# Three transformer blocks in one program: a joined change to the opening, the end, the norms, the linear attention's order, and the convolution's taps on quarters of TensorE

## The chip, the cores and the metric

The program runs on one NeuronCore of one Trainium2 chip. The metric is the device time in microseconds of one execution. The core's engines are TensorE (PE; its weight loads are listed apart as PEld), VectorE (DVE), ScalarE (ACT), GpSimd (POOL) and SyncE (SP), which issues nearly all DMAs. Each engine runs its own stream of instructions in order, and they meet through semaphores.

## What is computed

The input x is 256 tokens by 1024 features, float32. Two layers of a first model and one of a second follow, 8 stages in the kernel's count:

```python
# stages 0, 2, 3, 5: feed-forward;  1: even_mixer;  4: odd_mixer
for l in range(2):
    f = swiglu(rms_norm(h, g[0]), ffn1_w_in[l], ffn1_w_out[l])
    h = h + 0.5 * rms_norm(f, g[1])
    m = even_mixer(rms_norm(h, g[2]), ...) if l == 0 else odd_mixer(rms_norm(h, g[2]), ...)
    h = h + rms_norm(m, g[3])
    f = swiglu(rms_norm(h, g[4]), ffn2_w_in[l], ffn2_w_out[l])
    h = h + 0.5 * rms_norm(f, g[5])
# even_mixer: 8 heads of stick-breaking attention beside
c = u * sigmoid(gate)                      # 512 channels
c = causal_depthwise_conv(c, dw_w, dw_b)   # 31 taps for each channel
c = silu(layer_norm(c, ln_g, ln_b))
m = concat([attention, c]) @ hyb_w_out
# odd_mixer: gated linear attention, 4 heads
o = rms_norm(gla(q, k, v, g), norm_g);  m = (o * silu(r)) @ gla_w_out
# stages 6, 7: a second block (sparse attention, retention, gated feed-forward),
# its norms modulated by a scale and a shift, and at the end
out = rms_norm(x + gate2 * ffn, final_norm_w)
```

## The kernel before, in words

**Matrix products.** Every float32 weight matrix is streamed from HBM in units of 1 MB (`load_unit`, L429), three buffers `raw` deep. A unit holds two sub-blocks of 2 x 128 rows by 512 columns. For each, ACT rounds it to fp32r (`whi`, L460) and DVE makes the rest (`wlo`, L469). The activations are split alike into `xh` (ACT, L775) and `xl` (DVE, L770). PE then makes three products of 512 columns for each 128 rows: xh·whi (L571), xh·wlo (L572), xl·whi (L574). One sub-block for one half of the tokens (`tok` 0 or 1, 128 tokens) is a part (`pe_part`, L576): six matmuls. `act_begin` and `dve_begin` run the splits a few sub-blocks ahead.

**Order of work.** The order on every engine is written out by hand. At the entry of a stage (`pe_first`, L601) the parts of tok 0 come first while tok 1 is still being normed: PE transposes h (L743), DVE multiplies by the gain (L764), ACT and DVE split. The factor 1/rms (`rstd`) is applied later, when PSUM is read. It is made by ACT (sum of squares, L683) and by three POOL instructions: add the two halves (L697), scale and add epsilon (L690), power -0.5 (L692). In stages 6 and 7 (`pe_ada_x`, `act_ada_x`, `dve_ada_x`) it is applied before the transposes (L1681), then scale and shift (L1694, L1707).

**Opening (stage 0).** PE waits for the constants, transposes the norm gains (L555) and x (L743). DVE and ACT make all of tok 0's `xh` and `xl`, then split four sub-blocks; PE does parts 0 to 3 of tok 0, and tok 1's transposes before part 3.

**Stage 1 (`pe_hyb`, L1112).** The convolution has 4 blocks of 128 channels by 31 taps. A tap is either one DVE instruction (L1241, `Y += w_k * shifted x`) or one PE matmul with a diagonal 128x128 weight matrix that POOL made (L1108, L1311). PE has 38 taps (block 3, and 7 of block 2, `NT = 24`), DVE 86. All are float32, and a float32 matmul leaves two records in the trace. PE's taps stand in six groups between the attention's steps: weights (L1059, L1060), values (L1077, L1078, two heads on the two halves of PE's columns), scores (L1021, L1029, L1033, two heads on the two halves of PE's rows). Then come the mean (L1096), the variance (L1096 again), rsqrt and silu on ACT (L1223 to L1232), and the product with `hyb_w_out` (`pe_down`), whose part 4 is the first to need the silu's result.

**Stage 4 (`pe_gla`, L1473).** The scores of the chunked linear attention are made in 9 levels. `GLA` (L1342) is the hand-written order of their steps in 12 slots, one before each part pair of projections 3 to 6: "a" (POOL, differences), "e" (ACT, exp), "m" (DVE or POOL, times q and k), 0 and 1 (PE's two dots, L1391, and DVE's masked copies, L1435). After projection 6, eight heads' outputs (L1505, L1508) are made one to a PSUM bank, squared, normed (L1641), gated (L1644), transposed (L743) and split.

**End.** For each tok: DVE multiplies by the gate row (L1770), adds h (L1773), ACT squares, POOL makes rstd, DVE scales two halves (L2439), SP stores each (L2500).

## Time and profile before

| | |
|---|---|
| device time, median of 3 runs | 1450.81 us (1449.68 to 1451.09) |
| the profiled execution's own time | 1449.5 us |
| its span, first to last instruction | 1447.7 us |
| PE busy | 1418.4 us, 98% |
| DVE, ACT, POOL busy | 945.8, 720.4, 165.5 us |
| mean DMA rate | 198 GB/s |

In the rows below a time is in us from the span's start. A timeline row has start, length, engine, line, operation, out<-in, shapes, count, and in brackets the idle time before it and what ended it. Consecutive instructions of one form are merged (x8). Matmuls are pipelined, so the length of one (0.39) is longer than the step to the next (0.23). What a matmul costs in a stream is that step, or the whole of a merged row by its count.

### The profile page before, as it was taken

What the parts mean: (1) busy time and instruction counts of PE and PEld (TensorE: products, weight loads), DVE (VectorE), ACT (ScalarE), POOL (GpSimd) and SP (SyncE); (2) the same over time, 40 slices, a digit from 0 to 9 for tenths busy, and PEclk for the clock granted to TensorE, in tenths of its full rate; (3) what the DMA queues carried; (4) which work ended last, traced back from release to release, by engine and by line L of the source; (5) the groups of instructions that cost most, each with busy time, mean ns of one, the idle gap of its engine ahead of it and who ended that gap; (6) DMA issues with size and microseconds to landing.
All of it is one profiled execution on the core that took longest, in us unless ns stands there. A gap on an engine that the chain in (4) does not pass through costs nothing.

```text
span 1447.7 us, 17857 instructions
## 1 busy us (share of the span) xinstructions
PE 1418.4 (98%) x6695; PEld 1170.0 (81%) x6695; DVE 945.8 (65%) x1321; ACT 720.4 (50%) x1054; POOL 165.5 (11%) x262
## 2 busy tenths in 40 slices
PE   7999999999999999999999999999999999999997
PEld 5888888778888888888888888887877788788886
DVE  5666667777665677665786776665468566655543
ACT  5454455565444455543754544445555634544442
POOL 1900010010000010000162100001542110100000
PEclk9999999999999999999999999999999999999999
DMA  8685755246876778768533588674845355465551
GB/s 282 201 256 202 261 198 202 66 145 191 247 231 214 251 233 260 244 216 263 204 121 124 169 222 264 229 238 144 216 161 204 118 175 174 160 204 175 182 207 62
DMA packets 236341, 286.50 MB, mean 198 GB/s; under 512 B 37028, under 2 KB 160464, under 8 KB 236256
## 3 DMA queue, kind: packets, MB, share of 16 engines
q1 hardware_dynamic: 236000, 285.25, 61.1%
q8 instruction: 53, 0.87, 0.2%
q14 instruction: 32, 0.26, 0.1%
q10 hardware_dynamic: 256, 0.11, 0.0%
HBM read 281.13 MB, written 4.20 MB: 197 GB/s over the span
## 4 chain that ended last, share of the span: by engine, by line
PE 91%; ACT 3%; DVE 3%; DMA 2%; issue 2%; POOL 0%; ACTq 0%; DVEq 0%; POOLq 0%
PE ps L571 28%; PE ps L574 27%; PE ps L572 27%; PE ps L857 2%; DMA raw<-in_w_in_dram 1%; PE ps L1108 1%; PE ps L743 1%; ACT whi L460 1%; DVE wlo L469 1%; PE ps L1391 1%; PE ps L1059 0%; ACT junk L683 0%; PE ps L996 0%; ACT xh L775 0%; DMA fold<-in_norm_g_dram 0%
## 5 line engine op out<-in xcount | busy, mean ns | idle before, releaser
L469 DVE TENSOR_TENSOR wlo<-raw,whi 128x1024 fp32r<-128x1024 f32 (+2 forms) x474 | 563.1, 1222 | 243.9 <-ACT whi L460 243.5
L460 ACT ACTIVATE whi<-raw 128x1024 fp32r<-128x1024 f32 (+2 forms) x474 | 471.9, 1042 | 235.7 <-PE ps L574 95.3
L571 PE MATMUL ps<-whi,xh 128*128 128x512 f32 (+2 forms) x1440 | 567.9, 394 | 9.2 <-DVE wlo L469 6.7
L572 PE MATMUL ps<-wlo,xh 128*128 128x512 f32 (+2 forms) x1440 | 555.4, 386 | 0.0
L574 PE MATMUL ps<-whi,xl 128*128 128x512 f32 (+2 forms) x1440 | 548.3, 386 | 0.0
L571 PEld LDWEIGHTS ps<-whi,xh 128*128 128x128 f32 x1440 | 271.0, 188 | 67.8 <-DVE wlo L469 9.3
L574 PEld LDWEIGHTS ps<-whi,xl 128*128 128x128 f32 x1440 | 270.7, 188 | 55.6
L572 PEld LDWEIGHTS ps<-wlo,xh 128*128 128x128 f32 x1440 | 271.2, 188 | 50.7
L571 PE MATMUL ps<-whi,gh 128*128 128x512 f32 x440 | 172.6, 392 | 0.0
L572 PE MATMUL ps<-wlo,gh 128*128 128x512 f32 x440 | 171.3, 389 | 0.0
L574 PE MATMUL ps<-whi,gl 128*128 128x512 f32 x440 | 153.5, 389 | 0.0
L697 POOL TENSOR_TENSOR st<-st 128x1 f32<-128x1 f32 x30 | 8.2, 272 | 1094.9 <-ACT junk L683 1094.3
L838 ACT ACTIVATE hid<-ps,st 128x256 f32<-128x256 f32 x88 | 41.4, 471 | 126.2 <-PE ps L574 124.9
L574 PEld LDWEIGHTS ps<-whi,gl 128*128 128x128 f32 x440 | 82.6, 188 | 17.4
L572 PEld LDWEIGHTS ps<-wlo,gh 128*128 128x128 f32 x440 | 82.7, 188 | 16.7
L571 PEld LDWEIGHTS ps<-whi,gh 128*128 128x128 f32 x440 | 82.6, 188 | 16.7
L844 DVE SCALAR_TENSOR_TENSOR hid<-ps,st,hid 128x256 f32<-128x256 f32 x88 | 42.2, 479 | 62.2 <-ACT hid L838 62.2
L868 DVE TENSOR_TENSOR gl<-ps,gh 128x512 fp32r<-128x512 f32 x55 | 38.0, 691 | 67.1 <-ACT gh L863 67.1
L863 ACT ACTIVATE gh<-ps 128x512 fp32r<-128x512 f32 x55 | 32.9, 598 | 74.7 <-PE ps L857 74.7
L489 DVE SCALAR_TENSOR_TENSOR adaacc<-adat,scol,adaacc 128x512 f32<-128x512 f32 x84 | 62.9, 748 | 0.0
L775 ACT ACTIVATE xh<-xtmp 128x512 fp32r<-128x512 f32 x32 | 19.4, 634 | 32.9 <-DVE xtmp L764 32.7
L1311 POOL TENSOR_SCALAR diag<-cst,vcol 128x128 f32<-128x128 f32 x38 | 34.1, 916 | 7.9 <-DVE vcol L562 7.9
(239 smaller groups left out, 915.7 us busy)
## 6 DMA issues: line engine op xcount, KB each, us to landing
raw<-in_ffn_w_in_dram SPq DMA_DIRECT2D x174, 512.0 KB, 5.4
raw<-in_ffn_w_out_dram SPq DMA_DIRECT2D x40, 1024.0 KB, 5.7
raw<-in_w_in_dram SPq DMA_DIRECT2D x26, 1024.0 KB, 4.9
adat<-in_w_ada_dram SPq DMA_DIRECT2D x96, 256.0 KB, 2.9
raw<-in_w_ffn_gate_dram SPq DMA_DIRECT2D x22, 512.0 KB, 3.9
raw<-in_w_ffn_up_dram SPq DMA_DIRECT2D x22, 512.0 KB, 4.9
raw<-in_hyb_w_in_dram SPq DMA_DIRECT2D x10, 1024.0 KB, 5.5
raw<-in_gla_w_in_dram SPq DMA_DIRECT2D x10, 1024.0 KB, 5.1
```

The source lines that it names most:

```text
L460: e.activation(split_of(whi, j), raw_of(j), ACT.Copy).then_inc(*whi_made.up(j))
L469: e.tensor_tensor(split_of(wlo, j), raw_of(j), split_of(whi, j).bitcast(F32), ALU.subtract).then_inc(*wlo_made.up(j))
L489: e.scalar_tensor_tensor(adaacc[:, :], adat[n % 2][:, :], sc, adaacc[:, :], ALU.mult, ALU.add).then_inc(*ada_added.up(c, k))
L571: e.matmul(ps[:, 0:n], a, whi_of(j, k), start=first and k == 0, stop=False)
L572: last = e.matmul(ps[:, 0:n], a, wlo_of(j, k), start=False, stop=False)
L574: last = e.matmul(ps[:, 0:n], b, whi_of(j, k), start=False, stop=final and k == subs[j][2] - 1)
L838: e.activation(hb[:, tok * 512 + 256:tok * 512 + 512], acc.of(st, J0[st] + 4 * c, tok)[:, 0:256], ACT.Silu, scale=rstd(("h", st, tok)) if ...
L844: e.scalar_tensor_tensor(hb[:, tok * 512:tok * 512 + 256], acc.of(st, J0[st] + 4 * c, tok)[:, 256:512], rstd(("h", st, tok)) if st < 7 els ...
L857: last = e.transpose(ps[:, j * 256 + tok * P:j * 256 + (tok + 1) * P], hb[:, tok * 512 + j * P:tok * 512 + (j + 1) * P], ident)
L863: e.activation(gh[:, c * 512:(c + 1) * 512], tb.of("hid", st, c)[:, :], ACT.Copy).then_inc(*ghi_made.up(st, c))
L868: e.tensor_tensor(gl[:, c * 512:(c + 1) * 512], tb.of("hid", st, c)[:, :], gh[:, c * 512:(c + 1) * 512].bitcast(F32), ALU.subtract).then_i ...
L1311: e.tensor_scalar(diag[:, i * P:(i + 1) * P], ident, conv_w(b, k), None, ALU.mult).then_inc(*diag_made.up(i))
```

## The change

- **Opening.** PE runs 10 float32 matmuls on a tile of ones before the gains' transposes and 4 after the first x transposes (`pe_warm`). ACT's table set is loaded at once. Sub-blocks 0 and 1 are split before the second half of tok 0's `xh` and `xl`; tok 1 is turned before part 1, and the parts alternate between tok 0 and tok 1. The first part starts with the products that need only `whi` and `xh` (`pe_opening`).
- **Norms.** POOL's three instructions become two; the scale is put into ACT's squares.
- **Convolution.** PE takes 42 taps (`NT = 20`), DVE 82. A tap is two matmuls of 64 rows by 64 columns. Taps of even number use the quarters (rows 0-63, columns 0-63) and (64-127, 64-127) and sum in one PSUM bank, the odd ones the two other quarters and a second bank with its halves swapped. ACT copies the second bank, and two more matmuls with the identity swap it back into the first (`pe_taps_join`). The variance is asked for one pair of parts earlier (`i == 2`).
- **Linear attention.** Step (1, "m") moves from slot 4 to slot 3. ACT makes all Abs before Exp and Ln. The outputs go two heads to a bank, are made before parts 2 and 3 of projection 6, and half of tok 0's operand is transposed there; DVE gates two heads at once.
- **Stages 6 and 7.** `xh` and `xl` are made and waited for in four pairs of blocks, not two halves.
- **End.** The last tok's first half is multiplied by the gain ahead and scaled by ACT, which stores it through its own queue, beside DVE and SP with the other half.

The core of the diff:

```diff
+        def pe_warm(e, n):
+            e.wait_ge(*ones_set.at())
+            for _ in range(n):
+                e.matmul(acc.tiles[5][:, 0:P], ones[:, :], ones[:, :], start=True, stop=True)
...
-            lead = {0: 4, 6: 7, 7: 7}.get(st, 6)
+            lead = {6: 7, 7: 7}.get(st, 6)
...
-                return order + [(i, tok) for i in range(4, 8) for tok in range(2)]
+                return [(0, 0), (1, 0), (0, 1), (1, 1)] + [(i, tok) for i in range(2, 8) for tok in range(2)]
...
         def pool_rstd(e, key, factor=1.0):
-            e.tensor_tensor(v, ss[:, 0:1], ss[:, 1:2], ALU.add).then_inc(*rstd_step.up(key, 0))
-            e.wait_ge(*rstd_step.at(key, 0))
-            pool_power(e, v, 1, 1.0 / D, key, factor)
+            e.tensor_scalar(wk, ss[:, 0:1], ss[:, 1:2], EPS * factor ** -2, ALU.add, ALU.add
+                            ).then_inc(*rstd_step.up(key, 1))
+            e.wait_ge(*rstd_step.at(key, 1))
+            e.tensor_tensor(rk, wk, mhalf[:, 0:1], ALU.pow).then_inc(*rstd_made.up(key))
...
-        NT = 24
+        NT = 20
...
-                t = e.matmul(tb.of("conv")[:, (b - 2) * 256:(b - 1) * 256], diag[:, i * P:(i + 1) * P], cx_of(b, k),
-                             start=i == 0, stop=k == 30, skip_group_check=True)
+                ps = tb.of("convx" if i % 2 else "conv")
+                for p in (slice(0, 64), slice(64, P)):
+                    q = slice(64 - p.start, P - p.start) if i % 2 else p
+                    t = e.matmul(ps[q, (b - 2) * 256:(b - 1) * 256], diag[p, i * 64:(i + 1) * 64], cx_of(b, k)[p, :],
+                                 start=i < 2, stop=i % 2 == 1 and k >= 29, skip_group_check=True)
...
+        def pe_taps_join(e):
+            e.wait_ge(*convx_made.at())
+            for p in (slice(0, 64), slice(64, P)):
+                q = slice(64 - p.start, P - p.start)
+                t = e.matmul(tb.of("conv")[q, :], ident[p, p], hid[1][p, 0:512], start=False, stop=True,
+                             skip_group_check=True)
+            t.then_inc(*conv_sum.up())
...
+            pe_taps(e, PE_TAPS[36:42])
             pair(pe_values, 2)
-            pe_taps(e, PE_TAPS[32:38])
             pair(pe_values, 3)
+            pe_taps_join(e)
...
+            e.wait_ge(*conv_dot.at())
+            e.activation(hid[1][:, 0:512], tb.of("convx")[:, :], ACT.Copy).then_inc(*convx_made.up())
             act_values(e, 2)
-            e.wait_ge(*conv_dot.at())
+            e.wait_ge(*conv_sum.at())
...
-        GLA = [(1, "m"), (4, "a"), (3, "e"), (2, "m")]
+        GLA = [(4, "a"), (3, "e"), (2, "m"), "-"]
...
+                    if c == 6 and i >= 2:
+                        for hp in range(2):
+                            pe_gla_out(e, i - 2, hp)
+                    if c == 6 and i == 3:
+                        operand(0, 0)
...
+            e.activation(h[:, D:D + 512], xtmp[:, 0:512], ACT.Copy, scale=rstd(("h", 8, 1))).then_inc(*out_scaled.up())
+            e.wait_ge(*out_scaled.at())
+            e.dma_start(out[0, P:2 * P, 0:512], h[:, D:D + 512]).then_inc(*s_out_act.up())
```

## Rows read from the trace of the kernel before

**Rows 1.** The page: busy time by engine, and the granted clock in 40 slices.

```profile
PE 1418.4 (98%) x6695; PEld 1170.0 (81%) x6695; DVE 945.8 (65%) x1321; ACT 720.4 (50%) x1054; POOL 165.5 (11%) x262
...
PEclk9999999999999999999999999999999999999999
```

**Rows 2.** Waits of PE: engine, line, releaser: us in total, times, longest.

```profile
PE ps L571 <- DVE wlo L469: 6.7, 5, 3.7
PE ps L555 <- DMA fold<-in_norm_g_dram: 4.9, 1, 4.9
PE ps L743 <- ACT hid L1681: 2.5, 3, 1.1
PE ps L571 <- ACT xh L1232: 2.0, 2, 1.7
PE ps L1391 <- DVE gX L1420: 1.7, 1, 1.7
...
PE ps L743 <- DVE gr L1644: 1.1, 1, 1.1
```

**Rows 3.** Timeline of the opening, all engines.

```profile
5.09 1.91 PE L743 MATMUL ps<-cst,h 128*128 128x128 f32 x8
...
6.99 0.63 ACT L775 ACTIVATE xh<-xtmp 128x512 fp32r<-128x512 f32 x1 [4.06 <-DVE xtmp L764]
...
8.30 1.99 ACT L460 ACTIVATE whi<-raw 128x1024 fp32r<-128x1024 f32 x2
9.37 2.36 DVE L469 TENSOR_TENSOR wlo<-raw,whi 128x1024 fp32r<-128x1024 f32 x2 [0.26 <-ACT whi L460]
...
10.65 0.80 PE L571 MATMUL ps<-whi,xh 128*128 128x512 f32 x1 [3.65 <-DVE wlo L469]
...
13.38 0.63 PE L571 MATMUL ps<-whi,xh 128*128 128x512 f32 x1
...
13.81 0.63 PE L572 MATMUL ps<-wlo,xh 128*128 128x512 f32 x1
```

**Rows 4.** Timeline of PE around 26 us.

```profile
25.83 0.50 PE L571 MATMUL ps<-whi,xh 128*128 128x512 f32 x1 [1.30 <-DVE wlo L469]
```

**Rows 5.** Timeline of PE in stage 1: scores, taps, weights, values.

```profile
254.00 0.70 PE L1029 MATMUL ps<-qT,kT 64*128 64x256 f32 x4
...
261.79 3.62 PE L1108 MATMUL ps<-cx,diag 128*128 128x256 f32 x16
265.24 0.81 PE L1059 MATMUL ps<-mb,cst 128*128 128x384 f32 x2
...
271.40 0.66 PE L1077 MATMUL ps<-eb,vt 128*64 128x256 f32 x4
```

**Rows 6.** Chain that ended last, transposes of stage 1's entry (start, us, what).

```profile
198.97 0.87 PE ps L743 x8
```

**Rows 7.** Timeline of DVE in stage 1.

```profile
265.21 10.37 DVE L1241 SCALAR_TENSOR_TENSOR Y<-cx,vcol,Y 128x256 f32<-128x256 f32 x26
...
293.29 0.42 DVE L1287 TENSOR_TENSOR Y<-ps,Y 128x256 f32<-128x256 f32 x1
```

**Rows 8.** Timeline of PE at the end of stage 1: the mean, part 4.

```profile
294.48 1.89 PE L1096 MATMUL ps<-Y,ones 128*128 128x256 f32 x8
...
307.95 0.47 PE L571 MATMUL ps<-whi,xh 128*128 128x512 f32 x1 [1.68 <-ACT xh L1232]
```

**Rows 9.** Timeline of PE in stage 4: the outputs.

```profile
785.21 2.32 PE L1505 MATMUL ps<-gv,gS 128*128 128x256 f32 x10
```

**Rows 10.** Timeline of POOL at stage 7's entry: one rstd.

```profile
1246.14 0.19 POOL L697 TENSOR_TENSOR st<-st 128x1 f32<-128x1 f32 x1 [63.65 <-ACT junk L683]
1246.41 0.19 POOL L690 TENSOR_SCALAR st<-st 128x1 f32<-128x1 f32 x1
```

**Rows 11.** Timeline of the end.

```profile
1443.82 1.41 DVE L2439 SCALAR_TENSOR_TENSOR h<-h,st,row 128x512 f32<-128x512 f32 x2 [1.97 <-POOL st L692]
1444.60 0.99 SPq L2500 DMA_DIRECT2D out_dram<-h  x2
```

More of the change, by code:

```diff
@@ L616, in pe_first, with pe_opening @@
                         e.wait_ge(*done)
-                new = (xhi_made.at(st, tok, k // 2), xlo_made.at(st, tok, k // 2)) if c == 0 and k % 2 == 0 else ()
-                pe_part(e, bank[c, tok], j0 + i, xh, xl, 2 * k, 8, tok, *new)
+                new = ()
+                if c == 0 and (st >= 6 or k % 2 == 0):
+                    x = (st, tok, k if st >= 6 else k // 2)
+                    new = xhi_made.at(*x), xlo_made.at(*x)
+                if (st, i, tok) == (0, 0, 0):
+                    pe_opening(e, bank[c, tok], *new)
+                else:
+                    pe_part(e, bank[c, tok], j0 + i, xh, xl, 2 * k, 8, tok, *new)
+        def pe_opening(e, ps, hi, lo):
+            n = subs[0][3]
+            e.wait_ge(*whi_made.at(0))
+            e.wait_ge(*hi)
+            for k in range(2):
+                e.matmul(ps[:, 0:n], x_block(xh, k, 0), whi_of(0, k), start=k == 0, stop=False)
+            e.wait_ge(*lo)
+            for k in range(2):
+                e.matmul(ps[:, 0:n], x_block(xl, k, 0), whi_of(0, k), start=False, stop=False)
+            e.wait_ge(*wlo_made.at(0))
+            for k in range(2):
+                last = e.matmul(ps[:, 0:n], x_block(xh, k, 0), wlo_of(0, k), start=False, stop=False)
+            last.then_inc(*mm[0].up(0))
         def pe_chunk(e, st, j0, readers, at=None):
@@ L1275, in dve_hyb @@
             logs(1)
-            some(26)
+            some(20)
+            logs(2)
             dve_values(e, 0)
-            logs(2)
             some(6)
@@ L1281, in dve_hyb @@
             dve_values(e, 1)
-            some(8)
+            some(11)
             dve_values(e, 2)
@@ L1515, in pe_gla, with pe_gla_out @@
                     if q % 4 == 0 else (),
-                    lambda tok, n: [(squares, ("f", 4, tok), n), (f_scaled, 4, tok, n)], late=lambda: operand(1),
+                    lambda tok, n: [(squares, ("f", 4, tok), n), (f_scaled, 4, tok, n)], second, late,
                     lag=LAG[4], then=entry(e, 5))
+        def pe_gla_out(e, tok, hp):
+            ps = acc.next(("out", tok, hp), (gla_gated, tok, hp))
+            for done in acc.freed:
+                e.wait_ge(*done)
+            if (tok, hp) == (0, 0):
+                e.wait_ge(*lv_put.at(7, 1))
+                e.wait_ge(*lv_put.at(8, 0))
+                e.wait_ge(*gla_in.at(4, 1))
+            for hd in (2 * hp, 2 * hp + 1):
+                z = ps[:, hd % 2 * 256:hd % 2 * 256 + 256]
+                t = e.matmul(z, gS[:, hd * 256 + tok * P:hd * 256 + (tok + 1) * P],
+                             gv[:, tok * D + hd * 256:tok * D + (hd + 1) * 256], start=hd % 2 == 0, stop=tok == 0,
+                             skip_group_check=True)
+                if tok:
+                    t = e.matmul(z, gOFF[:, hd * P:(hd + 1) * P], gv[:, hd * 256:(hd + 1) * 256],
+                                 start=False, stop=True, skip_group_check=True)
+            t.then_inc(*gla_dot.up(tok, hp))
         def pe_gate_dot(e, hp):
@@ L1594, in act_gates @@
                                  ACT.Abs, bias=vector("bg", hd)).then_inc(*gate_abs.up(hd))
+            for hp in range(2):
                 x = slice(hp * 512, (hp + 1) * 512)
@@ L1691, in act_ada_x, with hi, affine @@
             e.wait_ge(*x_turned.at(st, tok, 1))
-            e.wait_ge(*xlo_made.at(*((st, 0, 1) if tok else (st - 1, 1, 1))))
-            for b in range(4, 8):
+            e.wait_ge(*xtmp_read(st, tok, 1))
+            def hi(g, ready):
+                e.wait_ge(*ready)
+                e.activation(x_pair(xh, g, tok), xtmp_pair(g), ACT.Copy).then_inc(*xhi_made.up(st, tok, g))
+            def affine(b):
                 e.activation(ada_part(1)[:, b - 4, :], of_4(tb.of("x", st, tok, 1))[:, b - 4, :], ACT.Identity,
@@ L1710, in dve_ada_x @@
             between()
-            for q in range(2):
-                dve_xlo(e, st, tok, q, ada_part(q))
+            for g in range(4):
+                e.wait_ge(*xhi_made.at(st, tok, g))
+                e.tensor_tensor(x_pair(xl, g, tok), xtmp_pair(g), x_pair(xh, g, tok).bitcast(F32), ALU.subtract
+                                ).then_inc(*xlo_made.up(st, tok, g))
         def act_ada_open(e, st, first):
```

318 lines of the change are left out of this document (191 added, 127 removed).

## The prediction

> **What bounds the kernel now.** I read the page's busy times first: PE is busy 1418.4 of 1447.7 us, every other engine far less [rows 1]. So a gain must either take work off PE or close one of its gaps, and those are 29.3 us in all. Next the waits of PE: they name nearly all of the gaps outside the end, 22 us, and each has one place [rows 2]. Then the timelines around those places [rows 3 to 5, 7 to 9, 11] with their lengths. The sum goes against the profiled execution's own 1449.5 us; the median of the runs is 1.3 us higher, and I add that at the end. A difference under 0.2% (2.9 us) is about what a measurement of this kernel can't tell from none.
>
> **Opening: 4.3 us gained.** Before, PE's first product starts at 10.65, since DVE and ACT first make all of tok 0 and wlo. Its matmuls then start 0.43 us apart (13.38 to 13.81), where a 512-column matmul later steps by 0.23; the clock line shows 9 for this slice too, but 512 columns in 0.43 us is the level of 1.2 GHz, and PE had stood idle 3.65 us before [rows 1, 3]. At 25.83 it has done 8 parts and tok 1's transposes, after another 1.3 us wait [rows 4]. After: the ten warm matmuls are 20 records of about 0.24 us (the x transposes at this clock: 1.91 over 8 [rows 3]), from about 1.0 to at most 5.8, up to 0.9 us behind the landed gains (4.87, the wait in [rows 2]). If they bring the clock up, the four x transposes behind them cost 0.44 and not 0.96 us, so DVE starts about where it did, 6.1 to 6.5. Then ACT: half of xh 0.63, whi 1.0 each; DVE: 0.7 for a half, wlo 1.2 each [rows 3]. In the new order whi 0 is there at 8.5, wlo 0 at 9.8, wlo 1 at 10.9, tok 1's xl at 13.6 and 14.3, wlo 2 at 15.8, wlo 3 at 16.9. PE: part (0,0) 8.6 to 10.3, transposes, (1,0) to 12.7, (0,1) held by xl to 14.3, (1,1) to 15.7, (2,0) at 15.8, from there six matmuls of 0.227 a part without a gap: 8 parts are done at 21.3, not 25.83. That is 4.5; I take 4.3, with 2.5 (the clock stays low until 12) and 5 as ends. ACT's early table load costs nothing, it stands before ACT's first work in both. SP's queue keeps its order; its fifth unit waits for wlo 3, which comes 0.7 us later than before, and PE needs that unit only 10 us after it lands.
>
> **Taps on PE: 5.4 us gained.** A tap costs 0.43 now: 16 records from 261.79 to 265.24 are 8 taps [rows 5]. 38 taps are 16.4 us. What two matmuls on parts of the array do is in the same rows: the two heads' scores on the two row halves take 0.70 for 4 records of 256 columns, the two heads' values on the two column halves 0.66, while 16 in a stream take 3.62, so 4 would take 1.03 with the pipeline's tail. Halves of rows run beside each other, and halves of columns do, into the same bank. Four quarters at once are in no row. The upper bound for a pair of taps is four matmuls in turn, 1.73 us; the lower is one, 0.43. I take 0.43, since both kinds of halves overlap fully: 21 pairs are 9.1. The join's two matmuls of 512 columns, twice a tap's, are 0.87 beside each other. The array's form changes 7 times more than before, each about 0.15 (0.70 less the 0.60 that two full overlapped records and a tail would be, and as much on the way out), 1.1. Sum 11.1 against 16.4: 5.3 to 5.4.
> The trace's own steps say that the halves overlap freely. The Trainium skill (TensorEngine Tiling (Array Packing), Restrictions and Gotchas) says that different row tiles can't access one PSUM bank at the same time. Here both matmuls of a tap are on different rows and in one bank, though in different partitions. By that rule a pair of taps would be 0.87 and the sum 9.1 us less; it is the first rival.
>
> **Is DVE ready?** If PE comes earlier, DVE's chain is next. A tap costs it 0.40 (26 in 10.37), and it ended at 293.29, just ahead of the mean at 294.48 [rows 7, 8]. From 261.4 it had 56 taps, 22.4, beside some 5.5 of logs, values and join, and 4.8 of waiting. After it has 52, 20.8. Laid out with the new counts and PE's new times it waits only 0.7 for `act_values(2)` (now behind ACT's 0.6 us copy of the second bank), and joins block 2 at 289.4; PE asks at 288.7. So 0.8 us of PE's gain waits there: 5.0 gained at the mean.
>
> **Variance a pair of parts earlier: 2.1 us.** From the sum of the variance to part 4's operand lie ACT's Ln, Exp, a table load and silu; part 4 waited 1.68, part 5 about 0.3 [rows 2, 8]. Asked 2.7 us (two parts) earlier, the chain ends 0.5 ahead of part 4. The squares are ready: mean at 289.5 to 291.3, DVE's wlo until 292.2, centring and squares to 294.1, while PE comes at 294.0 and needs the last of them 1.3 later. ACT has one whi fewer ahead of Ln; the whi that goes behind has 5 us until it is needed. If it were late, 2 us come back: ends 0 and 2.3.
>
> **Linear attention: 2.8.** (1, "m") stood behind a wlo that waited for ACT; at slot 3 DVE is free about 2 us before PE comes, so 1.7 to 1.9 go [rows 2]. Behind it, levels 2 to 6 shift with PE; the 0.6 at level 6 stays. Both Abs first: DVE's second pair 0.65 earlier, 0.65 gained. The outputs are the same 12 matmuls of 0.43 and 16 transposes, moved ahead of the last parts, so no work goes (10 records in 2.32, [rows 9]). The wait of 1.1 for gating [rows 2] goes, but the silu of `gr` is now behind the last part, and gating head pairs 0 and 1 come after it: by DVE's lengths gate (0,1) is there at 793.0, and PE asks for it at 792.1. I count 0.3. Ends: 1.3 and 4.
>
> **Norms and stages 6, 7: 1.2.** One of three POOL steps goes, 0.27 [rows 10]. It counts only where PE waits for it: stages 2 and 6 once, 7 twice (one with POOL slow, 0.4), from the 2.5 us of waits on L1681 [rows 2]. The pairs make four ACT and DVE instructions of half the length out of two; PE doesn't wait for the first half there, so nothing, and ACT ends 0.4 later, covered by DVE's. Ends: 0.3 and 2.
>
> **End: 0.9.** DVE's two scalings in turn, 1.41 [rows 11], become one beside ACT's: 0.7. One POOL step, 0.27. The product with the gain ahead costs DVE up to 0.1 on the path. The store issues at 1444.35 and not 1445.26, on two queues. Ends: 0.3 (ACT's queue lands later) and 1.1.
>
> **Sum.** 4.3 + 5.0 + 2.1 + 2.8 + 1.2 + 0.9 = 16.3. 1449.5 - 16.3 = 1433.2, and 1.3 to the median: 1434.5 us.
>
> **Rivals.**
> Half overlap (15%). The quarters run two at a time, by bank or because PE can't be fed: a pair of taps needs 8 loads and 8 matmul records, and the densest stream shown is 8 of each in 0.87 us, the transposes [rows 6]. Either gives 0.87 a pair, 9.1 us back: 1443.6. For it: nothing shows more than two at once. Against: the transposes' rate is set by their own columns, not by issue.
> A new wait eats part of it (10%). The mean waits for DVE's taps, or the opening's chain or gating slips by a step; 3 to 6 us back, about 1439.
> Slower (4%): the quarters don't overlap at all, at L1108. A pair is then 1.73, 21 times 1.3 is 27.3 back, and the join 0.4: 1462. It decides from a pair of 1.2 us (0.43 + 16.3/21) on. Against it: both kinds of halves overlap [rows 5].
> The opening does nothing (3%): if the gains' 0.9 us delay stays and the clock isn't up sooner, 4 us back, 1438.5.
> The forecast has 68%.
>
> **How the numbers follow.** The forecast's own ends are about 1431 and 1438; the wait and opening rivals lie in 1437 to 1441, half overlap at 1443.6. The range goes from 1431.0 to 1444.0, and leaves out the slower case and the tails. Faster by over 0.2%: all but the no-overlap case and a mixture near zero, 0.94; same 0.02; slower 0.04.
>
> **What would show it.** L1108: each group of taps should last 0.22 us a tap; 0.43 is half overlap, 0.87 none. The first product of PE near 8.6 and 0.23 steps from there; no gap at part (4,0). The waits for DVE gX L1420 and for ACT xh L1232 gone; a wait of under 1 us at the mean, for DVE, and one under 1 us at the transposes of `gr`. PE's busy time lower by about 5 only in stage 1. It would be wrong if PE waits at the mean for more than 2 us, or at stages that the change doesn't touch.

## The result, and the profile after

The changed kernel takes 1435.49 us, the median of 4 runs (1434.94 to 1436.08); the kernel before took 1450.24 us in the 4 runs beside them (1448.65 to 1451.09). The ratio is 0.9900 with a 95% interval of 0.9886 to 0.9915, so it is faster by more than the 0.2% that a measurement of this kernel can tell from none. The profiled execution took 1435.01 us, 14.5 us less than the one of before.

The page of the changed kernel, busy times and granted clock:

```profile
span 1433.2 us, 18097 instructions
...
PE 1415.5 (99%) x6819; PEld 1164.5 (81%) x6819; DVE 947.2 (66%) x1321; ACT 719.7 (50%) x1063; POOL 149.9 (10%) x237
...
PEclk9999999999999999999999999999999999999999
```

PE is 2.9 us less busy, although it now does 28 records of warming; the other 11.6 us were gaps. Of those gaps 3.9 us aren't saved but filled, since PE does its warming where it waited 4.9 us for the gains before, and now waits 1.0 for the tile of ones. Waits of PE after:

```profile
PE ps L776 <- ACT hid L1800: 2.3, 3, 1.0
PE ps L580 <- DVE wlo L472: 1.7, 3, 0.7
PE ps L1474 <- DVE gS L1518: 1.5, 1, 1.5
PE ps L553 <- DVE ones L2572: 1.0, 1, 1.0
PE ps L641 <- ACT whi L463: 1.0, 1, 1.0
PE ps L2398 <- ACT ar L2030: 0.7, 1, 0.7
```

Against [rows 2], the 4.9 us for the gains, 5 of the 6.7 us for wlo, the waits for `gX` of level 1 and for `xh` at part 4 are gone. (The first product, delayed before by the wait for wlo, now waits 1.0 us for `whi` instead.) One is longer: PE waits 1.5 us once for a level of the linear attention to be put away (L1474), where it waited 0.6.

**How the rest is read.** One number serves for the change and for all experiments: the start of the same group of matmuls in two traces, counted from the start of the span. I call the difference PE's lead. Before against after, by PE's timelines, it is

| group of matmuls (start in after, us) | PE's lead | what lies in this step |
|---|---|---|
| stage 1 (221.4) | 5.10 | opening 5.10 |
| sum of the mean (284.2) | 10.25 | taps 5.15 |
| entry of stage 2 (305.5) | 12.62 | variance 2.37 |
| gate's dot products in stage 4 (714.7) | 13.34 (12.66 just before) | Abs first 0.68 |
| level 1 (725.6) | 15.23 | its operand a slot earlier 1.89 |
| level 8 (758.5) | 14.05 | -1.18 |
| stage 5 (799.2) | 14.77 | outputs and gating 0.72 |
| stage 6, second entry (996.1) | 14.55 | -0.22 |
| PE's last record | 14.43 | -0.12 |
| span | 14.5 | end 0.1 |

The shares are read by place. The experiments below take back the warming, the crossed quarters, the split of the taps, the variance, level 1's slot, the pairs and the POOL step one by one. The order in the opening, both Abs first, and the outputs and gating have no run of their own; theirs are what is left at their place.

The opening after, all engines but the weight loads:

```profile
1.04 4.16 PE L553 MATMUL ps<-ones 128*128 128x128 f32 x20 [1.04 <-DVE ones L2572]
...
5.17 1.17 PE L776 MATMUL ps<-cst,h 128*128 128x128 f32 x8
...
6.61 0.63 ACT L815 ACTIVATE xh<-xtmp 128x512 fp32r<-128x512 f32 x1 [3.68 <-DVE xtmp L800]
...
8.23 0.72 PE L641 MATMUL ps<-whi,xh 128*128 128x512 f32 x2 [1.00 <-ACT whi L463]
...
8.80 0.63 PE L644 MATMUL ps<-whi,xl 128*128 128x512 f32 x2
```

The transposes of x take 1.17 us for 8 records, where they took 1.91 [rows 3], and the first product starts at 8.23 and not 10.65.

The taps in PE's timeline, in the place of [rows 5]:

```profile
256.77 2.39 PE L1175 MATMUL ps<-cx,diag 64*64 64x256 f32 x40
259.10 0.91 PE L1122 MATMUL ps<-mb,cst 128*128 128x384 f32 x2
...
261.03 1.96 PE L1175 MATMUL ps<-cx,diag 64*64 64x256 f32 x32
...
280.22 1.08 PE L1185 MATMUL ps<-hid,cst 64*64 64x512 f32 x4
```

40 records are 10 taps: each tap is two matmuls, on two quarters, of two records each. From 256.77 to the next group at 259.10 they take 2.33 us, or 0.23 a tap against 0.43 before.

### The profile page after: what moved, and what is told of

It is laid out like the page before. It is cut to its first block, busy times and chain, and to the rows that moved or that the text cites. A ratio compares the mean times of both kernels' runs of the same rounds, so it can differ in the third digit from the quotient of the medians.

```text
span 1433.2 us, 18097 instructions
## 1 busy us (share of the span) xinstructions
PE 1415.5 (99%) x6819; PEld 1164.5 (81%) x6819; DVE 947.2 (66%) x1321; ACT 719.7 (50%) x1063; POOL 149.9 (10%) x237
## 4 chain that ended last, share of the span: by engine, by line
PE 91%; DVE 4%; ACT 2%; issue 1%; DMA 1%; POOL 0%; POOLq 0%; ACTq 0%; DVEq 0%
PE ps L580 28%; PE ps L583 28%; PE ps L581 27%; PE ps L915 2%; DVE wlo L472 1%; DMA raw<-in_w_in_dram 1%; PE ps L776 1%; PE ps L1474 1%; PE ps L1175 1%; ACT whi L463 1%; PE ps L1122 0%; DVE h L1917 0%; DVE ps L1914 0%; PE ps L553 0%; PE ps L1059 0%
## 5 line engine op out<-in xcount | busy, mean ns | idle before, releaser
L580 PE MATMUL ps<-whi,xh 128*128 128x512 f32 (+2 forms) x1438 | 566.3, 394 | 2.7 <-DVE wlo L472 1.7
L580 PEld LDWEIGHTS ps<-whi,xh 128*128 128x128 f32 x1438 | 270.2, 188 | 60.6 <-DVE wlo L472 4.1
L580 PE MATMUL ps<-whi,gh 128*128 128x512 f32 x440 | 172.6, 392 | 0.0
L727 POOL TENSOR_SCALAR st<-st 128x1 f32<-128x1 f32 x30 | 12.7, 424 | 1098.4 <-ACT junk L713 1098.4
L580 PEld LDWEIGHTS ps<-whi,gh 128*128 128x128 f32 x440 | 82.6, 188 | 16.6
L713 ACT ACTIVATE junk<-h 128x512 f32<-128x512 f32 x36 | 22.4, 626 | 22.5 <-DVE h L1917 21.1
L915 PEld LDWEIGHTS ps<-cst,hid 128*128 128x128 f32 x220 | 27.3, 139 | 7.1
```

The source lines that it names most:

```text
L580: e.matmul(ps[:, 0:n], a, whi_of(j, k), start=first and k == 0, stop=False)
L713: e.activation(spare[:, 0:src.shape[1]], src, ACT.Square, scale=scale, accum_out=col(2, "ss", key)[:, i:i + 1]).then_inc(*squares.up(key, i))
L915: last = e.transpose(ps[:, j * 256 + tok * P:j * 256 + (tok + 1) * P], hb[:, tok * 512 + j * P:tok * 512 + (j + 1) * P], ident)
```

## The experiments

Each experiment was timed beside the kernel before, whose own median lay between 1450.2 and 1452.7 us on these occasions. So a run is read by its ratio to the kernel before beside it, not by its time, and above all by PE's position. This table gives the start of the same groups less that in the changed kernel's profile, in us; each part of the program has its column, so that an edit shows as a step between two of them.

| run | 221.4 | 284.2 | 305.5 | 725.6 | 758.5 | 984.7 | 996.1 | 1027.5 | 1035.1 | last |
|---|---|---|---|---|---|---|---|---|---|---|
| e1_cold | 1.21 | 1.21 | 1.19 | 1.18 | 1.18 | 1.14 | 1.14 | 1.76 | 4.69 | 4.74 |
| e2_straight | 0.97 | 9.96 | 9.96 | 9.98 | 10.29 | 10.25 | 10.25 | 10.23 | 10.72 | 10.77 |
| e3_var3 | 0.45 | 0.48 | 2.97 | 2.83 | 3.15 | 3.13 | 3.13 | 3.11 | 3.22 | 3.25 |
| e4_nt24 | 0.58 | 1.30 | 1.30 | 1.30 | 1.65 | 1.60 | 1.62 | 1.61 | 2.71 | 2.85 |
| e5_m4 | 0.56 | 0.57 | 0.54 | 2.55 | 1.40 | 1.43 | 1.44 | 1.42 | 4.97 | 5.12 |
| e6_dvem | 0.66 | 0.66 | 0.64 | 0.63 | -0.91 | -0.92 | -0.91 | -0.94 | -0.57 | -0.53 |
| e7_halves | 0.68 | 0.68 | 0.66 | 0.67 | 1.00 | 0.97 | 0.65 | 0.65 | 2.23 | 2.35 |
| e8_norm3 | 0.08 | 0.08 | 0.06 | 0.07 | 0.37 | 0.36 | 0.44 | 0.44 | 1.75 | 1.94 |
| e9_gate_endsp | 0.95 | 0.95 | 0.91 | 0.91 | 0.91 | 0.88 | 0.88 | 0.85 | -0.08 | -0.06 |
| e10_best | 0.54 | 0.54 | 0.54 | 0.56 | -1.00 | -0.96 | -1.29 | -1.29 | -2.26 | -2.26 |
| e12_best_w8 | -0.05 | -0.05 | -0.07 | -0.06 | -1.26 | -1.21 | -1.53 | -1.57 | -2.50 | -2.38 |

Three steps stand in many rows, whatever was edited. In the opening it is up to 1 us. Between 725.6 and 758.5 it is 0.3 us, in e2, e3, e4, e7 and e8 alike, whose edits don't touch these levels, and nothing in e1 and e9; so a step at the levels is known to some 0.3 us only. Between 1027.5 and 1035.1 it is 0.1 to 3.6 us, a finding of its own, under e9_gate_endsp.

### Without the warming matmuls

```
-            pe_warm(e, 10)
             pe_vectors(e, (0,))
...
-                pe_warm(e, 4)
```

> The changed kernel without its 14 warming matmuls; the opening's new order stays. The opening gained 5.05 us in all. Theory A (the clock has a part in it): the transposes of x take 1.9 us for 8 again and the matmuls from about 8.5 on step by 0.43 us until the clock rises, so PE comes to stage 1 between 0.5 and 1.5 us later than in the changed kernel (226.49 us in the trace of before, 221.44 in that of after; here 222.0 to 223.0), and the time is about 1436.4 us. Theory B (the new order made all of the gain, since PE waits for DVE's remainders until about 15 us anyway): stage 1 within 0.3 us of 221.44, time within 0.3 us of the changed kernel. Theory C (the clock is nearly all of it): 4 us or more back, about 1439.5.

Measured: 1439.24 us, ratio 0.9908 (0.9891 to 0.9926). PE comes to stage 1 1.21 us later than in the profile of after. Its opening:

```profile
4.95 0.42 PE L564 MATMUL ps<-cst,fold 96*128 96x96 f32 x1 [4.95 <-DMA fold<-in_norm_g_dram]
...
5.17 1.91 PE L776 MATMUL ps<-cst,h 128*128 128x128 f32 x8
...
8.69 1.22 PE L641 MATMUL ps<-whi,xh 128*128 128x512 f32 x2 [1.61 <-ACT whi L463]
...
9.71 1.05 PE L644 MATMUL ps<-whi,xl 128*128 128x512 f32 x2
```

The transposes are back at 1.91 us, and two 512-column records last 1.05 to 1.22 us instead of 0.63 to 0.72: that is the level of 1.2 GHz again, and it lasts until 11.4 us, where the next eight transposes take 1.20 us. The profile's granted clock reads 1.00 for all of this stretch in both kernels, so the level is read from the steps alone. Theory A holds: the clock is 1.2 of the 5.1 us in this pair, and the order has the other 3.9, by difference. The run's time is 3 us above the expected 1436.4 for another reason: PE's step of 2.9 us between 1027.5 and 1035.1, which other runs have too. Set against the other profiles with warming and the same opening, which lie 0 to 1.0 us behind that of after, the warming as it stands is worth 0.2 to 1.2 us.

### All taps on the straight quarters

```
-                    q = slice(64 - p.start, P - p.start) if i % 2 else p
+                    q = p
...
-                q = slice(64 - p.start, P - p.start)
+                q = p
```

> The changed kernel with every tap of the convolution, and the join, on the two straight quarters (rows 0 to 63 onto partitions 0 to 63, rows 64 to 127 onto 64 to 127), never on the crossed ones; banks, instructions and sums are the same. Theory A (four quarters work at once, and the gain is this overlap): a tap takes 0.43 us instead of 0.22, PE comes to the mean 42 x 0.215 = 9.0 us later (about 293.3 us in the trace) and the time is 9 us longer, about 1444.5. Theory B (what sets the pace is the issue of 8 short records a pair, not the quarters): the taps still take 0.22 to 0.3 us, and no more than 3 us come back.

Measured: 1445.44 us, ratio 0.9953 (0.9935 to 0.9971). The first ten taps in its timeline of PE:

```profile
257.74 4.54 PE L1175 MATMUL ps<-cx,diag 64*64 64x256 f32 x40
262.21 0.91 PE L1122 MATMUL ps<-mb,cst 128*128 128x384 f32 x2
```

The same 40 records take 4.47 us to the next group instead of 2.33, and PE loses 8.99 us from stage 1 to the mean; I had expected 9.0. Theory A holds: the records are as many, as short and as far from each other in the program, so issue doesn't set the pace, and the gain is that the crossed quarters work beside the straight ones. (All matmuls of a pair of taps, on four quarters, take 0.47 us. The two of one tap on two quarters take 0.45, about what one full matmul took, so two quarters at a time overlap fully here as well.)

### The variance at part 3

```
-                if i == 2:
+                if i == 3:
                     pe_total(e, "var", sq_of, lambda b: y_square.at(b), (y_ln,))
```

(and in the same way where ACT and DVE take their part.)

> The changed kernel with the sum of the variance asked at part 3 again, not at part 2. Theory A (the chain Ln, Exp, table, silu behind that sum ends last for part 4): part 4 waits again, some 1.9 to 2.4 us, and the time is 2.1 us longer, about 1437.6. Theory B (with the taps and the mean 5 us earlier the chain has room in either place): under 0.5 us.

Measured: 1438.62 us, ratio 0.9908 (0.9892 to 0.9923). The step from the mean to stage 2 is 2.49 us, and the waits of PE between 280 and 310 us are again

```profile
PE ps L580 <- ACT xh L1311: 2.0, 2, 1.7
```

as in [rows 2]. Theory A.

### Four taps back on DVE

```
-        NT = 20
+        NT = 24
...
-            pe_taps(e, PE_TAPS[36:42])
+            pe_taps(e, PE_TAPS[36:38])
```

> The changed kernel with 4 taps of block 2 moved from PE back to DVE (38 on PE as in the kernel before, in pairs). Theory A (DVE is next at the mean: its join of block 2 ends at 284.8 in the trace of after, where PE asks for it about 285.1): PE saves 4 x 0.215 = 0.86 us, DVE's join comes 1.6 us later, so PE waits some 2.2 us inside the mean's sum, and the variance comes 1.3 us later than in the changed kernel; time about 1436.8. Theory B (DVE has room): the 0.86 us of PE are gained, about 1434.6.

Measured: 1436.9 us, ratio 0.9898 (0.9879 to 0.9916), which can't be told from the changed kernel's. PE is 0.87 us earlier at the end of its taps (0.58 to -0.29 at 278.7 us) and then loses 1.59 at the mean, where the trace has a new wait:

```profile
PE ps L1159 <- DVE Y L1320: 1.6, 1, 1.6
```

Theory A holds in kind; the net loss is 0.72 us, not 1.3, since I had counted the wait as 2.2 us. It shows that DVE is next at the mean, and that `NT = 20` is better than 24 by 0.7 us of PE's time; a split with still fewer taps on DVE wasn't run.

### Level 1's operand a slot later

```
-        GLA = [(4, "a"), (3, "e"), (2, "m"), "-"]
+        GLA = [(1, "m"), (4, "a"), (3, "e"), (2, "m")]
...
-    ... [(0, 0), (0, 1), (2, "e"), (1, "m")]][i]
+    ... [(0, 0), (0, 1), (2, "e")]][i]
```

> The changed kernel with level 1's operand step of the linear attention put back one slot, to where it stood in the kernel before (at the head of the next chunk, behind a wlo that waits for ACT). In the traces PE gained 1.93 us at level 1 and lost 0.9 of it at level 7, where DVE's and POOL's steps overlap longer. Theory A (both are true of this edit): PE loses 1.7 to 1.9 us at level 1 and gets 0.9 back at level 7, so the time is about 1.0 us longer, 1436.5. Theory B (the loss at level 7 comes from elsewhere): the full 1.9 us are lost, 1437.4. Theory C (levels absorb it): under 0.3 us.

Measured: 1439.4 us, ratio 0.9913 (0.9898 to 0.9928). PE loses 2.01 us at level 1 and has 1.15 of it back at level 8: net 0.86. Theory A, so the slot gained 1.9 us and the levels behind it gave back over half (1.15 us, of which the 0.3 us seen in unrelated runs is the uncertainty). The rest of this run's distance isn't the edit's: it stands at 1035.1.

### Levels 6 and 8 multiplied on DVE

```
                 if n % 2:
-                if n % 2:
+                if n % 2 or n >= 6:
                     e.tensor_tensor(... gKT ..., ALU.mult).then_inc(*lv_kd.up(n))
...
-            if j == "m" and n % 2 == 0:
+            if j == "m" and n % 2 == 0 and n < 6:
```

> The changed kernel with the multiplication by k of levels 6 and 8 moved from POOL to DVE. In the trace of after PE waits 1.5 us at 754.7 for DVE's put of a level, and DVE's steps there take 1.77 and 2.30 us where POOL works beside them, against 0.68 and 1.21 alone. Theory A (POOL beside it stretches DVE's steps): DVE takes on 2 x 0.65 us and loses the stretch of about 2.2 us, so the wait shrinks by 0.5 to 0.9 us, time about 1434.8. Theory B (DVE is short of time as such): the wait grows by up to 1.3 us, time up to 1436.8.

Measured: 1435.25 us, ratio 0.9889 (0.9872 to 0.9905). PE gains 1.54 us between levels 1 and 8, and L1474 is no longer among its waits. DVE in the changed kernel:

```profile
745.93 0.63 DVE L1495 COPY gX<-gB 128x512 f32<-128x512 f32 x1
746.49 1.77 DVE L1503 TENSOR_TENSOR gX<-gX,gQT 128x512 f32<-128x512 f32 x1
748.18 2.30 DVE L472 TENSOR_TENSOR wlo<-raw,whi 128x1024 fp32r<-128x1024 f32 x1
```

POOL at the same time:

```profile
744.28 2.00 POOL L1529 TENSOR_TENSOR gX<-gB 128x512 f32<-128x512 f32 x1 [4.70 <-PE ps L1474]
746.25 3.15 POOL L1538 TENSOR_TENSOR gX<-gX,gKT 128x512 f32<-128x512 f32 x2
```

And DVE in this run, where POOL ends at 746.92 (one step of 2.02 us from 744.90) and does nothing beside the rows shown:

```profile
747.12 0.68 DVE L1501 TENSOR_TENSOR gX<-gX,gKT 128x512 f32<-128x512 f32 x1
747.72 0.68 DVE L1503 TENSOR_TENSOR gX<-gX,gQT 128x512 f32<-128x512 f32 x1
748.32 1.21 DVE L472 TENSOR_TENSOR wlo<-raw,whi 128x1024 fp32r<-128x1024 f32 x1
```

The same two DVE steps take 1.89 us and not 4.07 once POOL has nothing to do beside them; the step taken on costs 0.68. Theory A, and by more than I gave it: taking work on made DVE sooner done.

The kernel before shows why PE lost 1.18 us at these levels by the change. There the same two DVE steps fell into a pause of POOL's (762.50 to 764.01), and only the wlo ahead of them was stretched:

```profile
759.32 2.03 DVE L469 TENSOR_TENSOR wlo<-raw,whi 128x1024 fp32r<-128x1024 f32 x1
...
762.70 0.68 DVE L1420 TENSOR_TENSOR gX<-gX,gQT 128x512 f32<-128x512 f32 x1
763.30 1.21 DVE L469 TENSOR_TENSOR wlo<-raw,whi 128x1024 fp32r<-128x1024 f32 x1
```

That stretch was 0.8 us, and 0.3 on a copy; after the change it is 2.2. The slowing isn't always DVE's: in this run a wlo at 744.80 takes its usual 1.21 us beside POOL's step at 744.90, and POOL's takes 2.02, where the same step takes 1.07 us in the kernel before while DVE does nothing (753.15).

### Stages 6 and 7 in halves

```
-                if c == 0 and (st >= 6 or k % 2 == 0):
-                    x = (st, tok, k if st >= 6 else k // 2)
+                if c == 0 and k % 2 == 0:
+                    x = (st, tok, k // 2)
```

(and the four steps of pairs in `act_ada_x` and `dve_ada_x` are two steps of halves, as in the kernel before.)

> The changed kernel with the operands of stages 6 and 7 made in halves again, not in pairs of blocks. In the trace PE's lead over the kernel before falls by 0.25 us at 994 us, where it waits 0.35 us for ACT's squares of f, which stand behind ACT's eight steps of the operand instead of six. Theory A (the pairs cost this): PE gets 0.25 us back there, the time is 0.2 to 0.5 us shorter, about 1435.2. Theory B (the pairs gain something elsewhere in stages 6 and 7 that hides in the sum): 0.3 to 1 us longer.

Measured: 1437.37 us, ratio 0.9900 (0.9885 to 0.9915). PE gets 0.32 us back between 984.7 and 996.1, and nothing moves in stage 7 beyond what unrelated runs show (0.12 us from 1035.1 to the last record, 0.14 in e4). The wait of 0.3 us for ACT's squares (L580 for `junk`) is gone. Theory A: the pairs only cost, as far as these traces tell. The median can't show 0.3 us; the position can.

### The norm in three steps

```
-            e.tensor_scalar(wk, ss[:, 0:1], ss[:, 1:2], EPS * factor ** -2, ALU.add, ALU.add
-                            ).then_inc(*rstd_step.up(key, 1))
+            e.tensor_tensor(v, ss[:, 0:1], ss[:, 1:2], ALU.add).then_inc(*rstd_step.up(key, 0))
+            e.wait_ge(*rstd_step.at(key, 0))
+            e.tensor_scalar(wk, v, 1.0, EPS * factor ** -2, ALU.mult, ALU.add).then_inc(*rstd_step.up(key, 1))
```

> The changed kernel with the sum of the two halves of each norm as a POOL step of its own again (three steps, not two). Theory A (the step is on PE's path in stages 2, 6 and 7 and at the end, as I predicted): 0.17 to 0.27 us at each of some five places, 0.7 to 1.3 us longer, about 1436.4, and PE's lead in stages 6 and 7 falls by 0.2 us at each wait for the norm. Theory B (PE's waits there end with something else, or the new step with two column operands is as long as the two old ones): under 0.3 us in all.

Measured: 1437.43 us, ratio 0.9900 (0.9886 to 0.9915). PE loses nothing at stage 2, 0.08 us at stage 6 and some 0.16 at stage 7's entry (1.82 at 1216.6 us, 1.98 at 1233.7). With 0.14 us at the end that is some 0.4 us in all, between the two theories (under 0.3, and 0.7 to 1.3) and nearer to B: PE's waits hardly hang on this step. The end of the changed kernel shows why a step of 0.28 us is worth so little:

```profile
1427.99 0.19 ACT L713 ACTIVATION_READ_ACCUMULATOR junk<-h 128x1 f32 x1
1428.28 0.30 POOL L727 TENSOR_SCALAR st<-st 128x1 f32<-128x1 f32 x1 [5.85 <-ACT junk L713]
1428.66 0.56 POOL L730 TENSOR_TENSOR st<-st,mhalf 128x1 f32<-128x1 f32 x1
```

The step with two operands from columns takes 0.30 us and not 0.19, and starts 0.29 after the read and not 0.26: from the read to the power's end it is 1.23 us, against 1.37 in the kernel before (1442.42 to 1443.79; its steps at stage 7 are [rows 10]). One step less is 0.14 us.

### A store of 4 KB moved, and the end on one queue

```
-                if u in (U0[5] + 10, U0[6] + 8):
+                if u in (U0[5] + 10, U0[6] + 15):
```

(and the dma_start of the half that ACT scales stands in SP's program, behind the other one.)

> The changed kernel with two edits at places far apart in the trace. First, the store of the second gate row (1024 single elements of 4 bytes, 14 us from issue to landing) is issued 7 units of weights later in stage 6 (after unit 15, not 8). In all traces so far PE's lead over the other kernels stays constant within 0.1 us except between 1027 and 1036 us, where ACT waits 6.2 to 9.2 us for weights whose loads were issued just behind this store, and PE loses 0.2 (after) to 3.5 us (level 1 put back) by run. Theory A (this store holds up the weights, and makes most of the difference from run to run): no run-to-run loss at 1027 to 1036 and PE's wait of 0.7 to 2 us for ACT there is gone; 0.4 us or more gained against the changed kernel's profiled run, more at the median, and the spread of the runs is smaller. Theory B (the weights of stage 6 are late as such): the waits stay. Second, at the end the half that ACT scales is stored from SP's queue as well, not from ACT's. Theory A (the 512 KB that are left at 1430.0 set the end: at 400 GB/s they take 1.3 us after 1.1 us of start): 2.6 to 2.8 us from the last issue to the end as before the edit. Theory B (a second queue is slow to start): 2.1 us, 0.5 us gained.

Measured: 1434.72 us (1434.12 to 1434.99), ratio 0.9886 (0.9871 to 0.9901). Between 1027.5 and 1035.1 PE gains 0.93 us on the changed kernel's profile and up to 4.5 on other runs, and it has no wait there. e10_best and e12_best_w8, with the same move, gain 0.97 and 0.93. What it had run into, in the DMA view of the level-1 run, 1008 to 1030 us, in 40 slices of 0.55 us, and the issues with their median time to landing:

```profile
GB/s 395 238 0 0 0 127 298 402 350 387 384 372 350 406 402 286 280 269 41 37 48 11 11 41 34 48 34 15 41 60 71 101 115 89 127 216 268 250 313 410
...
raw<-in_w_in_dram SPq DMA_DIRECT2D x5, 1024.0 KB, 13.0
...
gate_rows<-modc SPq DMA_DIRECT2D x1, 4.0 KB, 16.4
```

A store of 1024 separate elements needs 16.4 us, and for some 9 us of it (16 slices) all 16 engines together move 11 to 115 GB/s, where they move 269 to 406 just before and up to 410 after. The weights that are issued around it come late. In the run of this section the low rates move with the store, to 1052 to 1062 us (5 to 45 GB/s). The other odd transfer there, the load of a row of 512 KB at 1018 us, stays at its place and lands after 7.4 us instead of 16.4; so it is held up itself and isn't the cause. ACT's timeline, first of the changed kernel and then of the one without warming:

```profile
1022.50 2.01 ACT L463 ACTIVATE whi<-raw 128x1024 fp32r<-128x1024 f32 x2 [6.19 <-DMA raw<-in_w_in_dram]
```

```profile
1026.67 2.01 ACT L463 ACTIVATE whi<-raw 128x1024 fp32r<-128x1024 f32 x2 [9.21 <-DMA raw<-in_w_in_dram]
```

ACT's copies then stand ahead of the step that PE waits for. Seven units later in the stage the same store (at 1047.36) costs nothing: PE has no wait from 1008 to 1065 us.

In e1_cold and e5_m4 the late weights are only half of the loss. PE of e1_cold after its wait:

```profile
1035.11 0.44 PE L2397 MATMUL ps<-cst,ar 128*128 128x128 f32 x2 [1.99 <-ACT ar L2029]
...
1036.35 0.63 PE L580 MATMUL ps<-whi,xh 128*128 128x512 f32 x1
1036.78 0.63 PE L581 MATMUL ps<-wlo,xh 128*128 128x512 f32 x1
```

and the same stretch by windows (stretch, length, busy time of PE, PEld, DVE, ACT and POOL, granted clock, DMA share, GB/s):

```profile
1036.00:1037.00 1.00, 1.00 (x4) 0.81 (x3) 0.48 (x1) 0.77 (x2) 0.86 (x3) 0.50 1.02 389
```

The matmuls step by 0.43 us, and the granted clock is 0.50, the level of 1.2 GHz, from about 1035.7 to 1039.2; in e5_m4 it is the same from 1036.6 to 1040.1. That costs some 1.7 us in each, an estimate from 3.4 us at half speed. The waits cost the rest: 2.0 and 0.5 us in e1_cold and 2.7 in e5_m4, against 0.7 in the changed kernel. Together that is about 3.5 and 3.7 us, and the table has 3.55 and 3.53 from 996.1 to 1035.1. So a gap of 2 to 3 us in PE's work can cost as much again through the clock, but needn't: e7_halves waits 2.4 us at the same place and e8_norm3 2.1, and their clock stays at 1.00.

Theory A, as far as the traces go. The spread is told by four runs of each kernel alone: 0.9 us here, 1.1 for the changed kernel, 3.6 and 3.7 for e1_cold and e5_m4.

At the end the last store is issued at 1430.35 instead of 1430.03, the first at 1429.98 instead of 1430.00, and the span is 1433.1 us instead of 1433.2. DMA of the changed kernel from 1425 to the end, in slices of 0.2 us, and of the kernel before from 1440 on:

```profile
GB/s 400 370 250 0 0 0 0 0 0 0 0 0 0 0 0 0 0 0 0 0 0 0 0 0 0 0 0 0 110 420 370 400 370 420 360 110 0 0 0 0
...
out_dram<-h ACTq DMA_DIRECT2D x1, 256.0 KB, 2.7
out_dram<-h SPq DMA_DIRECT2D x1, 256.0 KB, 2.6
```

```profile
GB/s 96 0 0 0 0 0 0 0 0 0 0 0 0 0 0 0 0 0 0 0 0 0 0 0 0 0 0 0 266 415 372 362 383 394 394 139 0 0 0 0
...
out_dram<-h SPq DMA_DIRECT2D x2, 256.0 KB, 2.0
```

Both move 512 KB at about 390 GB/s, 1.35 us, and begin 0.8 to 0.9 us after the first issue (at 1430.00 here, at 1444.60 in [rows 11]). The queue is not what counts; theory A again.

### Four edits together

```
+                if n % 2 or n >= 6:          (levels 6 and 8 on DVE)
+                    x = (st, tok, k // 2)    (stages 6 and 7 in halves)
+                if u in (U0[5] + 10, U0[6] + 15):
+            for n in range(2):               (last halves scaled and stored in two pieces each)
+                e.activation(h[:, D + n * 256:...], xtmp[:, n * 256:...], ACT.Copy, ...)
+                e.dma_start(out[0, P:2 * P, n * 256:(n + 1) * 256], ...)
```

> The changed kernel with four edits together: the multiplication by k of levels 6 and 8 on DVE (measured 1.55 us gained at 758), stages 6 and 7 in halves (0.32 us at 996), the gate row's store 7 units later (0.4 us or more at 1030), and the last two halves scaled and stored in quarters of a row, so that the first bytes leave 0.3 us earlier. Theory A: all four add up, 2.5 us or more below the changed kernel, about 1432.5 or less, ratio to the kernel before about 0.987. Theory B for the end (what counts is the time of the last issue, not of the first byte): the two more instructions cost 0.1 to 0.2 us there.

Measured: 1432.55 us (1432.40 to 1432.67), ratio 0.9872 (0.9855 to 0.9888). The steps add up: 1.56 us at the levels, 0.33 in stage 6, 0.97 at 1035.1. At the end the span is 2.4 us below the changed kernel's and PE's last record 2.26, so the pieces gained 0.1, not 0.3. The first of them was issued at 1427.51, which is 0.2 us earlier against PE, but the last only at 1428.49, 0.7 us later. So the first byte alone doesn't set the end either: the last piece has to be there in time.

### The kernel before with the store moved

```
-                if u in (U0[5] + 10, U0[6] + 8):
+                if u in (U0[5] + 10, U0[6] + 15):
```

> The kernel before, with one edit alone: the store of the second gate row is issued after unit 15 of stage 6, not 8. It tells whether the hold-up of the weights at 1030 us belongs to both kernels. Theory A (it does, and makes the run-to-run spread of both): the runs lie within 1 us of each other (the kernel before: 1448.6 to 1453.9), the profiled one has no wait for ACT at L2252 (0.5 us in the profile of before), and the median is 0.5 to 1.5 us below the kernel before of the same call. Against it the changed kernel with the same move (1434.7) then has the change's own gain, 15 to 16 us. Theory B (the kernel before had the slack, and only the changed one ran into it): no difference in median or spread.

Measured: 1449.29 us (1448.65 to 1450.50, 11 runs) beside 1450.70 of the kernel before (1449.48 to 1451.53, 15 runs), ratio 0.9992 (0.9983 to 1.0001). In the trace the wait of 0.5 us at L2252 is gone, and PE gains 0.73 us there on the kernel before (the changed kernel's lead falls from 14.51 to 14.31 over the kernel before, and from 15.51 to 14.58 over this run). The time's interval just holds no difference, and the spread of 1.9 us misses the 1 us that I expected. So the hold-up belongs to both kernels by the trace; that it makes the spread of the kernel before isn't shown. With the store moved in both, the medians differ by 14.6 us (1449.29 and 1434.72; the kernels before beside them are 0.3 us apart), not by the 15 to 16 that I expected.

### Eight warming matmuls instead of ten

```
-            pe_warm(e, 10)
+            pe_warm(e, 8)
```

(on top of the four edits.)

> The version of the last combination (e10_best) with 8 warming matmuls ahead of the gains' transpose instead of 10. In the eleven profiles with 10, their 20 records last 3.9 to 4.6 us by run: where the clock comes up late they end at 5.67 us and hold the gains' transpose, landed at 4.95, until 5.46, and PE comes to stage 1 0.7 to 1.1 us later than in the profile of after; where it comes up early they cost nothing. Theory A (two fewer take away what stands in the way, and the clock comes up as before): the transpose starts at 4.95 to 5.1 us in any run, PE is at stage 1 0.4 us earlier than in the late runs (0 to 0.6 us behind the profile of after, against 0.7 in the last combination), median 1432.2 to 1432.5. Theory B (the two also bring up the clock): the transposes of x stay slow (1.9 us for 8), and 0.5 us or more is lost, as without any warming (1.25 us behind): 1433.

Measured: 1432.73 us (1432.49 to 1433.00), ratio 0.9868 (0.9852 to 0.9885). The gains' transpose starts at 4.96 and the transposes of x are fast:

```profile
1.04 3.78 PE L553 MATMUL ps<-ones 128*128 128x128 f32 x16 [1.04 <-DVE ones L2563]
...
4.96 0.30 PE L564 MATMUL ps<-cst,fold 96*128 96x96 f32 x1
...
5.10 1.17 PE L776 MATMUL ps<-cst,h 128*128 128x128 f32 x8
```

PE is 0.6 us earlier at stage 1 than in e10_best. With ten, seven of the ten profiles (not eleven, as I had counted) look like this one, of the straight quarters, where the warming ends late and the transpose starts at 5.46:

```profile
1.04 4.63 PE L553 MATMUL ps<-ones 128*128 128x128 f32 x20 [1.04 <-DVE ones L2572]
```

Theory A by this one profile; the median doesn't tell it from e10_best, so whether it holds from run to run is open. Both beat the changed kernel by some 0.3% of the time by their ratios. The intervals only just touch (e10_best up to 0.9888, the changed kernel from 0.9886) or miss each other (e12_best_w8 up to 0.9885).

## Why the prediction was right or wrong

The forecast, its range and its likeliest case came true: 1434.5 us predicted, 1435.5 measured. The mechanisms of the three largest gains, opening, taps and variance, are the ones given. But part of the nearness is luck. Of the six terms three came out larger than forecast (opening, mean, variance, by 1.2 us together) and three smaller (linear attention, norms, end, by 3.0), so the sum is 14.5 us and not 16.3. And the median lay only 0.5 us above the profiled run, not 1.3 as in the kernel before, which gave back 0.8 of these 1.8 us.

- **Opening, 4.3 predicted, 5.1 measured.** The mechanism is the one given, clock and order. DVE was a step faster than laid out, with the second tok's first product at 12.50 us and not 14.3. The delay by the warming matmuls that I feared is real, 0.4 us at the gains' transpose in seven of ten profiles, but not in the one of after. The rival that the opening does nothing is out.
- **Taps, 5.4 on PE and 5.0 at the mean; measured 5.15.** A pair of taps costs what one did; the rival of half overlap (9.1 us back) is what e2_straight makes, 9.0. So the place that I weighed against the Trainium skill (TensorEngine Tiling (Array Packing), Restrictions and Gotchas) went by the trace: two row tiles wrote one bank at the same time without loss, in different partitions. The step that failed is small: the 0.8 us wait for DVE at the mean didn't come, its join ended at 284.81 and PE has no wait there; with four taps more on DVE it does come (1.6 us). The prediction's own numbers don't meet here either: 5.4 less 0.8 is 4.6, while its 5.0 is 294.48 less 289.5. Four quarters into one bank I didn't try; the Trainium skill (PSUM — Partial Sum Buffer, PSUM bank collisions raise a hardware error) says that two row tiles that write into the same bank and the same quadrant, its word for 32 partitions, raise an error, which no run here shows.
- **Variance, 2.1; measured 2.4**, and 2.5 when taken back.
- **Linear attention, 2.8; measured 2.1.** Abs first 0.68 (0.65 predicted), level 1's slot 1.89 (1.7 to 1.9), the outputs 0.72 (0.3). The step that failed is the sentence that the levels behind shift with PE and that the 0.6 at level 6 stays: it grew, and 1.2 us went there, because DVE's steps and POOL's now lie on each other for longer (a stretch of 2.2 us on DVE, 1.1 before, by the rows under e6_dvem). e5_m4 and e6_dvem show both halves of it.
- **Norms and stages 6 and 7, 1.2; measured -0.3.** Two errors of mechanism. The POOL step was sized at 0.27 by its start-to-start time, while its successor is longer and later, which leaves 0.14, and of that PE got nothing at stage 2, 0.1 at stage 6 and 0.2 at stage 7 (e8_norm3). And I costed the pairs at nothing, with DVE as the cover for ACT's extra 0.4 us. The cover was the wrong one: behind ACT's eight steps stand its squares of the other half, and PE waits for their bank (0.3 us, e7_halves). The rest, 0.2 us, is the late weights at 1030.
- **End, 0.9; measured 0.1.** The last issue is 0.8 us earlier, nearly as predicted, at 1430.03 against 1430.83 (1445.26 less PE's lead of 14.43). But in the kernel before the two stores were already in flight behind each other, and 512 KB take 1.35 us from the first byte. The first issue moved by 0.2 us only (1430.00 against 1444.60 less 14.43, 1430.17), and the first byte by little more than 0.1 (by the two rows of GB/s under e9_gate_endsp). The step that failed is to have counted the last issue. I had named a late queue as the risk; it was the bytes.

## What to carry to other kernels

A chain that ends in a store ends with its bytes: count when the first of the last 512 KB leaves and how long they take, not only when the last instruction is issued. An engine step that shares its path with another engine's can be worth moving to the busier engine, and a freed slot upstream may only press the two on each other. Where runs of one kernel differ, compare positions in several traces by part of the program: here nearly all of it lay at three places, and the largest was a 4 KB store, with a fall of the clock behind it in two runs.
